# A decoder block on one core: modulation weights held stationary in the head, splits before the norm, a split forget row, and x reloaded in parts

## The reference, cut to what matters

```
cond = silu(c)
mod  = cond @ w_ada + b_ada -> shift1, scale1, gate1, shift2, scale2, gate2
h    = rms_norm(x, g_norm1) * (1 + scale1) + shift1
proj = h @ w_in             -> q, k, v, gates of both branches, forget logits
o_a  = gated linear attention, 4 heads
o_b  = forgetting attention, 16 heads:
       s = q k^T * scale + cum[query] - cum[key], causal softmax, @ v
merged = sigmoid(gate_a) * (o_a @ w_proj_gla) + sigmoid(gate_b) * (o_b @ w_proj_fox)
x = x + gate1 * (merged @ w_out)
x = x + gate2 * (relu(h2 @ w_ff1)^2 @ w_ff2),  h2 from x like h
out = rms_norm(x, g_final)
```

## Time and profile before

| | us |
|---|---|
| median of 3 runs | 1960.01 (1956.65 to 1961.27) |
| the profiled execution itself | 1956.35 |
| its span, first to last instruction | 1954.3 |
| PE busy | 1884.2 |
| DVE busy | 1195.6 |
| ACT busy | 836.3 |

### The profile page before, as it was taken

How to read it: one execution, slowest core, us unless ns; L and a number is a source line. 1 busy time by engine, 2 the same in 40 slices (tenths; PEclk the granted TensorE clock), 3 DMA queues, 4 the chain that set the end, 5 groups by cost and what they waited for, 6 DMA issues and landing times.

```text
span 1954.3 us, 21726 instructions
## 1 busy us (share of the span) xinstructions
PE 1884.2 (96%) x8451; PEld 1498.1 (77%) x8451; DVE 1195.6 (61%) x1458; ACT 836.3 (43%) x1050; POOL 34.9 (2%) x48
## 2 busy tenths in 40 slices
PE   6998999999999999999999997999999999999997
PEld 2447788788787887878888776788888888888885
DVE  5664655565666666756666667875555555555554
ACT  3214544444445445334433444444344344434443
POOL 1000000000000000000000000000000000000000
PEclk8999999999999999999999998999999999999998
DMA  9987678688888798799789787686666666666663
GB/s 365 310 294 178 190 177 212 193 218 196 217 192 219 238 202 253 227 273 248 252 247 244 227 271 239 216 272 206 192 191 184 194 193 184 188 194 190 185 190 119
DMA packets 232297, 428.89 MB, mean 219 GB/s; under 512 B 17834, under 2 KB 34266, under 8 KB 231555
## 3 DMA queue, kind: packets, MB, share of 16 engines
q1 hardware_dynamic: 231328, 423.99, 74.8%
q10 hardware_dynamic: 834, 3.50, 0.5%
q0 software_dynamic: 32, 0.02, 0.0%
HBM read 425.34 MB, written 2.10 MB: 219 GB/s over the span
## 4 chain that ended last, share of the span: by engine, by line
PE 45%; issue 34%; DMA 11%; DVE 7%; ACT 3%; SPq 0%; POOL 0%; POOLq 0%; ACTq 0%; DVEq 0%
PE ps L1455 37%; DMA raw<-in_w_in 5%; DVE wlo L986 3%; DMA raw<-in_w_out 2%; ACT whi L555 2%; PE ps L1411 2%; DVE acc L1026 1%; DMA raw<-in_w_ff 1%; DMA raw<-in_w_proj_fox 1%; PE ps L1566 1%; DMA first<-in_w_ada 1%; PE ps L1564 1%; DMA raw<-in_w_proj_gla 1%; PE ps L1439 0%; PE ps L1416 0%
## 5 line engine op out<-in xcount | busy, mean ns | idle before, releaser
L986 DVE TENSOR_TENSOR wlo<-raw,whi 128x1024 fp32r<-128x1024 f32 x608 | 748.9, 1235 | 664.9 <-ACT whi L555 662.4
L555 ACT ACTIVATE whi<-raw 128x1024 fp32r<-128x1024 f32 x608 | 642.7, 1060 | 970.4 <-PE ps L1455 586.4
L1455 PE MATMUL ps<-whi,hT 128*128 128x512 f32 x2304 | 746.3, 399 | 22.3 <-DVE wlo L986 17.8
L1455 PEld LDWEIGHTS ps<-whi,hT 128*128 128x128 f32 x2304 | 438.4, 190 | 140.4 <-issue 24.8
L1455 PE MATMUL ps<-wlo,hT 128*128 128x512 f32 x1152 | 453.7, 394 | 0.0
L1455 PE MATMUL ps<-whi,obT 128*128 128x512 f32 x1280 | 403.9, 394 | 4.1 <-DVE wlo L986 2.3
L1455 PE MATMUL ps<-whi,oaT 128*128 128x512 f32 x1280 | 398.9, 391 | 0.0
L1455 PEld LDWEIGHTS ps<-whi,obT 128*128 128x128 f32 x1280 | 242.0, 189 | 55.9 <-issue 3.0
L1455 PEld LDWEIGHTS ps<-whi,oaT 128*128 128x128 f32 x1280 | 240.4, 188 | 50.2 <-issue 0.5
L1455 PEld LDWEIGHTS ps<-wlo,hT 128*128 128x128 f32 x1152 | 219.7, 191 | 45.0 <-issue 1.4
L1455 PE MATMUL ps<-wlo,obT 128*128 128x512 f32 x640 | 250.5, 391 | 0.0
(11 more groups left out here) (209 smaller groups left out, 786.2 us busy)
## 6 DMA issues: line engine op xcount, KB each, us to landing
raw<-in_w_ff SPq DMA_DIRECT2D x256, 512.0 KB, 4.1
raw<-in_w_in SPq DMA_DIRECT2D x224, 512.0 KB, 5.8
raw<-in_w_ada SPq DMA_DIRECT2D x128, 512.0 KB, 5.2
first<-in_w_ada SPq DMA_DIRECT2D x64, 512.0 KB, 8.5
raw<-in_w_in SPq DMA_DIRECT2D x64, 256.0 KB, 5.1
raw<-in_w_proj_fox SPq DMA_DIRECT2D x32, 512.0 KB, 5.2
raw<-in_w_proj_gla SPq DMA_DIRECT2D x32, 512.0 KB, 4.9
raw<-in_w_out SPq DMA_DIRECT2D x32, 512.0 KB, 5.4
```

The lines of the kernel that those rows point to most:

```text
L555: nc.scalar.activation(whi[g % WRING][:], raw[POS_G[g] % RING][:], ACT.Copy).then_inc(s_hi, 1)
L986: V.tensor_tensor(wlo[g % WRING][:], raw[POS_G[g] % RING][:], whi[g % WRING][:].bitcast(F32), ALU.subtract).then_inc(s_lo, 1)
L1455: i = T.matmul(ps[bank(name, t)][:], src[:, kt, hl, tk], w[sl][:, k, :], start=(kt == 0 and n == 0), stop=(kt == KT - 1 and n == 2))
```

## The change

- `x` becomes SP's first load, ahead of its wait for `bi` and of all `first` tiles.
- `ada_first` and `sum_first` on PE hold 128 by 128 weights (or a block of `acc`) stationary and move one column (`cond`, or ones), four matmuls each, adding up directly in four columns of `ps[6]` or `ps[7]`, by turns. `row_first`, `tmp`'s use here and `cols_first` go away; `mod_first` reads the columns two places earlier (idx 9).
- On DVE the first `lo` of a pair's six units stands at idx 0, ahead of `norm1`, and the others at idx 1, 3, 5, 7, 10; on PE the six units stand at idx 1, 3, 5, 7, 10 and after idx 15. ACT's and SP's orders follow. After the last pair, `lo` of unit 18 stands ahead of `norm1(3)`.
- The forget row is split: DVE writes `nch` (float32r) and `ncl = nct - nch`, two POOL DMAs lay them on partitions 0 and 1, and `fox_scores` does one float32r matmul with two rows of ones for each block.
- `x` is reloaded in four parts of 512 KB, at u = 2, 9, 16 and 23.

The core of the diff:

```diff
-    ncrow = at("ncrow", [1, FH, S], r1)
+    ncrow = at("ncrow", [2, FH, S], r1, F32R)
...
+            sp.dma_start(x_in[:], x_v).then_inc(s_x, 16)
             sp.wait_ge(s_init, 1)
...
-                    if n >= 2 and idx % 2 == 1 and idx < 12:
-                        load(ROW_G * (n // 2 - 1) + idx // 2)
+                    if n >= 2 and idx in (1, 3, 5, 7, 10):
+                        load(ROW_G * (n // 2 - 1) + 1 + (1, 3, 5, 7, 10).index(idx))
+                    if idx == 14:
+                        load(ROW_G * (n // 2))
...
-            pool.wait_ge(s_fcd, 2)
-            nc.gpsimd.dma_start(ncrow[0:1, :, :], nct[:]).then_inc(s_rowcum, 16)
+            pool.wait_ge(s_fcd, 4)
+            nc.gpsimd.dma_start(ncrow[0:1, :, :], nch[:]).then_inc(s_rowcum, 16)
+            nc.gpsimd.dma_start(ncrow[1:2, :, :], ncl[:]).then_inc(s_rowcum, 16)
...
+            for i in range(ADA0 // 2):
+                for k in range(ROW_G if i < 3 else LEAD):
+                    hi(ROW_G * i + k)
+                    if k == 0:
+                        norm1_hi(i)
...
-                        act.dma_start(xl[:], x_v).then_inc(s_xl, 16)
+                        t, half = (u - 2) // 14, (u - 2) // 7 % 2 * (D // 2)
+                        act.dma_start(xl[:, t, half:half + D // 2], x_v[:, t, half:half + D // 2]).then_inc(s_xl, 16)
...
-                    if i and idx == 2:
+                    if i and idx == 0:
+                        lo(ROW_G * (i - 1))
                         norm1(i - 1)
...
+                V.tensor_copy(ones_r[:], ones[0:2, :])
+                V.tensor_copy(nch[:], nct[:]).then_inc(s_fcd, 1)
+                V.tensor_tensor(ncl[:], nct[:], nch[:].bitcast(F32), ALU.subtract).then_inc(s_fcd, 1)
...
-                T.matmul(ps[6][0:1, :], cond[:, 2 * mm + 1:2 * mm + 2], first[mm][:, 1, :],
-                         start=(mm == 0), stop=False).then_inc(s_adp, 1)
+                for j in range(4):
+                    i = T.matmul(ps[6 + n % 2][:, j:j + 1], first[mm][:, 1, j * P:j * P + P],
+                                 cond[:, 2 * mm + 1:2 * mm + 2], start=(mm == 0 and j == 0), stop=False,
+                                 skip_group_check=True)
+                i.then_inc(s_adp, 1)
...
-                T.matmul(ps[6][0:1, :], ones[:, 0:1], acc[:, n % 2, :], start=False, stop=True).then_inc(s_rowsum, 1)
-            def cols_first(n):
+                for j in range(4):
+                    i = T.matmul(ps[6 + n % 2][:, j:j + 1], acc[:, n % 2, j * P:j * P + P], ones[:, 0:1],
+                                 start=False, stop=(j == 3), skip_group_check=True)
+                i.then_inc(s_modmm, 1)
...
-                    if i and idx in (4, 6, 7, 10, 12):
-                        row_unit(ROW_G * (i - 1) + (4, 6, 7, 10, 12).index(idx))
+                    if i and idx in (1, 3, 5, 7, 10):
+                        row_unit(ROW_G * (i - 1) + (1, 3, 5, 7, 10).index(idx))
...
-                    i = T.matmul(ps[4][:, c0:c0 + keys], ones[0:1, :], ncrow[0:1, n, 0:keys],
+                    i = T.matmul(ps[4][:, c0:c0 + keys], ones_r[:], ncrow[:, n, 0:keys],
```

More of the change, by code:

```diff
@@ L190, in build @@
     nct = at("nct", [FH, S], gt + 7168)
+    nch = at("nch", [FH, S], gt + 5120, F32R)
+    ncl = at("ncl", [FH, S], gt + 6144, F32R)
+    ones_r = at("ones_r", [2, P], gt + 4096, F32R)
     tri = at("tri", [P, P], gt + 9216)
@@ L440, in _ @@
                     load_first(n, mm)
-                    if (n, mm) == (0, 3):
-                        sp.dma_start(x_in[:], x_v).then_inc(s_x, 16)
                     idx = UG * (n % 2) + mm
-                    if n >= 2 and idx % 2 == 1 and idx < 12:
-                        load(ROW_G * (n // 2 - 1) + idx // 2)
-            for pos in range(ROW_G * 3, len(STREAM)):
+                    if n >= 2 and idx in (1, 3, 5, 7, 10):
+                        load(ROW_G * (n // 2 - 1) + 1 + (1, 3, 5, 7, 10).index(idx))
+                    if idx == 14:
+                        load(ROW_G * (n // 2))
+            for pos in range(ROW_G * 3 + 1, len(STREAM)):
                 if pos == G_FOX:
@@ L824, in _ @@
                         gla_heads(4, u)
-                    if it == 1 and u == 2:
+                    if it == 1 and u in (2, 9, 16, 23):
                         act.wait_ge(s_oa, 16)
-                        act.dma_start(xl[:], x_v).then_inc(s_xl, 16)
+                        t, half = (u - 2) // 14, (u - 2) // 7 % 2 * (D // 2)
+                        act.dma_start(xl[:, t, half:half + D // 2], x_v[:, t, half:half + D // 2]).then_inc(s_xl, 16)
                     if it == 3 and u in (25, 27, 29):
@@ L944, in ada_first @@
                     if n > 1:
-                        dve.wait_ge(s_rowsum, n - 1)
+                        dve.wait_ge(s_modmm, n - 1)
                 else:
@@ L997, in _ @@
                         V.tensor_scalar(xn[:, 0, :], x_in[:, 0, :], nst[:, 5, 0:1], None, ALU.mult).then_inc(s_xnd, 1)
-                    if i and idx == 2:
+                    if i and idx == 0:
+                        lo(ROW_G * (i - 1))
                         norm1(i - 1)
-                    if i and idx % 2 and 3 <= idx < 15:
-                        lo(ROW_G * (i - 1) + (idx - 3) // 2)
-                    if idx == 11:
+                    if i and idx in (1, 3, 5, 7, 10):
+                        lo(ROW_G * (i - 1) + 1 + (1, 3, 5, 7, 10).index(idx))
+                    if idx == 9:
                         mod_first(2 * i)
             lo(ROW_G * 3)
+            norm1(ADA0 // 2 - 1)
             lo(ROW_G * 3 + 1)
-            norm1(ADA0 // 2 - 1)
             lo(ROW_G * 3 + 2)
@@ L1086, in forget_cums @@
                 V.tensor_scalar(nct[:], ps[6][0:FH, 0:S], -1.0, None, ALU.mult).then_inc(s_fcd, 1)
+                dve.wait_ge(s_ones, 1)
+                V.tensor_copy(ones_r[:], ones[0:2, :])
+                dve.wait_ge(s_fcd, 2)
+                V.tensor_copy(nch[:], nct[:]).then_inc(s_fcd, 1)
+                dve.wait_ge(s_fcd, 3)
+                V.tensor_tensor(ncl[:], nct[:], nch[:].bitcast(F32), ALU.subtract).then_inc(s_fcd, 1)
             halves = (slice(0, P), slice(P, 3 * P))
@@ L1408, in ada_first @@
                 pe.wait_ge(s_fraw[mm], 16 * (n + 1))
-                if mm == 0 and n:
-                    pe.wait_ge(s_row, n)
-                T.matmul(ps[6][0:1, :], cond[:, 2 * mm + 1:2 * mm + 2], first[mm][:, 1, :],
-                         start=(mm == 0), stop=False).then_inc(s_adp, 1)
+                if mm == 0 and n > 1:
+                    pe.wait_ge(s_mod, n - 1)
+                for j in range(4):
[3 more added lines that the diff above has]
+                i.then_inc(s_adp, 1)
             def sum_first(n):
                 pe.wait_ge(s_ada, (n + 1) * (2 * UG))
-                T.matmul(ps[6][0:1, :], ones[:, 0:1], acc[:, n % 2, :], start=False, stop=True).then_inc(s_rowsum, 1)
-            def cols_first(n):
-                pe.wait_ge(s_row, n + 1)
-                if n:
-                    pe.wait_ge(s_mod, n)
                 for j in range(4):
-                    m = T.matmul(ps[7][:, j:j + 1], tmp[0:1, j * P:j * P + P], ones[0:1, 0:1],
-                                 start=True, stop=True)
-                m.then_inc(s_modmm, 1)
+                    i = T.matmul(ps[6 + n % 2][:, j:j + 1], acc[:, n % 2, j * P:j * P + P], ones[:, 0:1],
+                                 start=False, stop=(j == 3), skip_group_check=True)
+                i.then_inc(s_modmm, 1)
             def bank_free(name, h):
@@ L1487, in _ @@
                         norm_turn(idx - 10)
-                    if i and idx in (4, 6, 7, 10, 12):
-                        row_unit(ROW_G * (i - 1) + (4, 6, 7, 10, 12).index(idx))
-                    if i in (1, 2) and idx == 15:
-                        row_unit(ROW_G * (i - 1) + 5)
+                    if i and idx in (1, 3, 5, 7, 10):
+                        row_unit(ROW_G * (i - 1) + (1, 3, 5, 7, 10).index(idx))
                 if i == 0:
@@ L1494, in _ @@
                     norm_turn(7)
-            cols_first(ADA0 - 1)
+                else:
+                    row_unit(ROW_G * (i - 1) + 5)
             for g in range(ROW_G * 3, G_FOX):
@@ L1558, in fox_scores @@
                 if n == 0:
-                    pe.wait_ge(s_rowcum, 16)
+                    pe.wait_ge(s_rowcum, 32)
+                    pe.wait_ge(s_fcd, 4)
                     pe.wait_ge(s_btd, 4)
```

16 lines of the change are left out of this document (2 added, 14 removed).

## The result

The changed kernel takes 1933.17 us (median of 4 runs, 1932.92 to 1940.80) against 1959.36 us before: a ratio of 0.9877, 95% interval 0.985 to 0.990. That is 26.2 us faster. The forecast was 1922.6 with a range of 1907 to 1938: the time lies in the range, but 10.6 us off the forecast, on the figure of the rival in which DMA or the clock eats the head's gain (1933).

The account below looks back on a forecast made before the run. PE, busy for 96% of the span, was taken as the bound outside idle stretches in the head and near 857 us. -23.7 - 7.2 - 6.5 = -37.4 from 1956.35 gives 1919.0; 3.66 above: 1922.6 us, range 1907 to 1938.

Parts of the forecast that it names:

- the rival in which DMA or the clock eats the head's gain: Rival: in the head, blocks of 33.8 us, two slow units a block, or both add 6 to 16 us; 1933 us; 20%.
- the head: The stretch from 0 to 157 us: its gains, less what DMA gives back, were to sum to -23.7 us.
- Stationary weights: In the head, the modulation's groups cost 0.9 to 1.0 us each (+2 us), and the turning goes (-5.9 us).
- the clock's share goes with them: In the head, the slow units behind PE's idle stretches go together with those stretches: -5.6 us.
- the first start: In the head, PE's first unit starts at 41.6 us instead of 45.72: -4.1 us.
- Splits ahead of the norm: In the head, PE's idle stretches between pairs of parts and after the last sum go: -13.1 us.
- DMA: In the head, loads come within 4% of PE, so a block takes 32 us, not 31.0: +3 us.
- The forget row: In the forget scores, a head takes 1.43 us instead of 1.88, over 16 heads: -7.2 us.
- x in parts: Near 857 us, loading x in four parts removes most of a 6.8 us loss on PE: -6.5 us.
- -2, were each part to make its own small stall: Bound on the gain near 857 us: only 2 us won if each of x's four parts stalls a little.
- Does not do what it says: Rival: in the head, `norm1` still ends last, so idle PE and clock stay; 1941 us; 5%.
- loads stand bare: Rival: in the head, weight load and column run in sequence, 3.5 us a group, not 0.95; about 2065 us; 4%.

Follow-up runs that it names:

- row form: The changed kernel, new order kept, but the modulation's eight parts computed as before (512 weights moving past cond's column, row copied and turned): 1930.20 us, ratio 0.9858.

## Why the prediction was right or wrong

*The number.* The profiled execution was forecast at 1919.0 and took 1932.92. In the stretches the head fell 10.6 us short and x 8.8, the forget scores gave 2.1 more, and 2.5 came where nothing was forecast. The forecast then added 3.66 us for the distance from that execution to the median; the changed kernel's median lies 0.25 above its own. That 1933.17 meets the rival's 1933 is partly luck: the rival was right on the head (two slow units a block, 10 us), and the failure of x, which no rival had, was covered by the scores, the unforecast 2.5 us and the 3.4 us of the median.

*Stationary weights.* The cost of a group at the upper clock was right: 0.79 to 0.95 us, 0.9 to 1.0 forecast. The step that failed is "the clock's share goes with them" (-5.6), with the first start beside it (-4.1). The sum priced the groups by rows in which a group stands alone between long matmuls, and took it that a PE which no longer idles keeps its clock. Both losses are in the trace, two slow units and their surroundings per block (1.6 + 0.5 + 2.5 + 0.2 = 4.8 us), and a first unit at 46.70 instead of 41.6; the kernel with 64 columns gives 11.5 us of them back at 263 with nothing changed but the moving width. That is shown, not argued. The 10.6 us missing in the head are 5.1 at the first unit, 5.2 up to unit 18, which starts at 146.5 (the sum gives 136.2; the "near 134" of the prediction leaves out its own 3 us for DMA), and 0.3 behind it. Why narrow matmuls let the clock fall is open. The window of 15 to 20 us that the rival of DMA or the clock cited the earlier trace rows was the hint; I set it aside because PE had been idle before it.

The Trainium skill ("TensorE: Matmul & The Clock Gate", section "Why this matters for your kernels") advises continuous PE work and warns of idle gaps. Here PE was busy in every one of the four windows shown and the clock was at 0.50 in one of them, so being busy was not enough.

*Splits ahead of the norm.* The idle stretches went, as forecast, with one-column and with 64-column groups. With 64 columns 0.9 to 4.0 us of idle PE come back for `first` tiles. But the gain was booked on one edit where two remove the same wait: of the 13.1 us of idle PE behind the first start, 2.7 are left with the stationary form alone and 5.0 with the new order alone. On top of the stationary form the order adds 2 to 4 us with the clock up; with one column it lines the groups up, three and four in a row, and adds nothing.

*The first start.* 41.6 was forecast; 41.27 (row form) and 42.03 (64 columns) measured. The chain was right where PE ran at full clock from 32 us on; in the changed kernel the transposes and groups ahead of the norm ran at half pace.

*DMA.* I took +3 us for it. In the changed kernel it costs nothing visible: no DMA stands in the chain from 46.70 to 168 us, since PE is slower than forecast; with the clock up it is the next bound, at 377 to 392 GB/s. The head as a whole: 23.7 forecast, 13.1 measured; with 64 columns 24.6, 23.9, 24.2, 22.7 and 22.5 in five executions.

*The forget row.* 1.41 us per head measured, 1.43 forecast; the 0.2 us at each change of row shape is there with two rows as well, if the matmul itself takes the 0.06 and 0.12 us that the prediction put in (no row shows the 0.06 alone). The term of the sum was 7.2, the stretch gave 9.3. The 1.8 us beside the matmuls go with a dip of the clock right behind one head's scores, which the kernel before has at 347 us. The three kernels without the split row have one, one and three such dips in this stretch and take 330.4, 330.5 and 333.7 us, some 1.7 us for each dip; no kernel with the split row has any, and why is open.

*x in parts.* -6.5 forecast, about +0.5 measured: the term failed entirely. The 6.8 us of stall were real, but they were not the price of the load. Without any load of x the stretch is 2.1 us shorter, not 6.8, since it has stalls of its own. The likely reading, not tested by itself, is that the single load took them all at once, as it held up tiles which would have been late in smaller steps. "-2, were each part to make its own small stall" was the bound nearest to the truth, and still too far out.

*Does not do what it says* and *loads stand bare*: both out; a pair takes 0.10 to 0.12 us at the upper clock.

The lowest times are those of the change with 64 moving columns and x in eight parts: 1918.63 and 1924.19 us in two measurements, ratios 0.980 and 0.9825, against 0.9877 for the change as it was. The other kernels with 64 columns and the new order (1924.11, 1926.15, 1926.42) are not told apart from it.

## What to carry to other kernels

When a matmul is turned round so that the weights stand and one column moves, its duration among long matmuls is not its whole price: look at what the clock does when many of them stand in a row, and try a wider moving operand, which cost less than 0.1 us a group here (0.84 us in the chain instead of 0.79) and gave 7 us back in all. When a stall is to be removed by splitting a transfer, first take the transfer away: only what that saves can be won. When two edits remove the same wait, run each alone before booking the gain on either.

## What the runs showed of the hardware that was not expected

- A PE that is busy in every microsecond, with 128-column weight loads and one moving column, drops to the lower clock (0.50 from 75 to 80 us), and runs at the lower pace from the start until the first long matmuls. It does not do so each time: in one of three executions with the same head the first block stayed at 1.00. The same loads with 64 moving columns keep the upper level there, but are at half pace until 31 us too (1.81 us a group).
- The clock column of a window reads 1.00 where the trace has no clock record yet, though durations are doubled (1.71 against 0.79 to 0.95 us for the same eight records).
- A float32r matmul of two rows and 128 or 256 columns takes 0.25 and 0.31 us in the chain, against 0.41 and 0.62 for the two passes of float32 with one row.
- With 64 moving columns one core's loads run at 373 to 392 GB/s in every window of 5 us from 65 to 110 us.
